# Conditioning pieces, chained token loads and a split projection in a two-layer diffusion step

## The reference

```python
for i in range(DEPTH):
    mp = adaln(c_ctx[None, :], mod_w[i], mod_b[i])      # silu(cond) @ w + b: 6 vectors
    ms = adaln(c, mod_w[i], mod_b[i])
    hp = rmsnorm(xp, norm_mix[i]) * (1.0 + mp[:, 1]) + mp[:, 0]
    ...
    op, st = rglru_mixer(hp, h0, *p)     # or chunk_mlp_mixer; out = (mixed * gate) @ w_out
    xp = xp + mp[:, 2] * op
    hp = rmsnorm(xp, norm_ffn[i]) * (1.0 + mp[:, 4]) + mp[:, 3]
    xp = xp + mp[:, 5] * swiglu(hp, ffn_w_gate[i], ffn_w_up[i], ffn_w_down[i])
```

## Time and profile before

| | us |
|---|---|
| median of 3 runs | 1532.39 (1531.67 to 1532.84) |
| the profiled execution | 1532.15 |
| its span, slowest core (6) | 1530.6 |
| TensorE busy | 1437.0 |
| VectorE busy | 906.6 |
| ScalarE busy | 650.6 |
| GpSimd busy | 225.7 |

### The profile page before, as it was taken

One profiled execution on the slowest core, in us unless ns is written; L12 is line 12 of the kernel. 1 busy time (PEld: TensorE's weight loads), 2 busy tenths in 40 slices (PEclk: granted clock), 3 DMA queues, 4 the chain that ended last, 5 costly groups with the idle time before them and its releaser, 6 DMA issues.

```text
span 1530.6 us, 20044 instructions; the slowest of 8 cores (1516.5 to 1530.6 us)
## 1 busy us (share of the span) xinstructions
PE 1437.0 (94%) x6971; PEld 661.7 (43%) x6971; DVE 906.6 (59%) x1316; ACT 650.6 (43%) x866; POOL 225.7 (15%) x377
## 2 busy tenths in 40 slices
PE   4978996899999999999999999999999999999997
PEld 2433443444444445444444444444444444444444
DVE  1578695458687646528863364538856447744446
ACT  2597996548888234632013032632125013201023
POOL 6011021135231210011111100011110000101000
PEclk9999998999999999999999999999999999999999
DMA  9998368499435873554646754353332535985303
GB/s 176 171 191 129 49 110 193 57 156 146 74 60 86 168 137 55 84 83 70 110 69 97 117 101 72 56 83 56 55 63 47 86 55 93 198 142 87 65 1 110
DMA packets 50182, 151.56 MB, mean 99 GB/s; under 512 B 5410, under 2 KB 11042, under 8 KB 49572
## 3 DMA queue, kind: packets, MB, share of 16 engines
q0 software_dynamic: 45312, 133.32, 53.2%
q1 hardware_dynamic: 4772, 16.96, 3.4%
HBM read 270.94 MB, written 8.42 MB: 183 GB/s over the span
## 4 chain that ended last, share of the span: by engine, by line
PE 79%; DMA 9%; ACT 5%; issue 4%; DVE 3%; POOL 0%; DVEq 0%; ACTq 0%; POOLq 0%
PE pb L110 78%; DMA ringF<-modw 4%; DMA x_fm<-lru_in 2%; ACT h L105 1%; ACT reg L105 1%; ACT L105 1%; DMA x_fm<-xin 1%; DMA ringM<-lru_in 1%; DMA ringF<-ffn_d 1%; DVE x_fm L112 1%; DVE tmpn L112 1%; DMA tff<-lru_w_out 0%; ACT FS L105 0%; ACT x_fm L105 0%; DMA ringM<-lru_w_out 0%
## 5 line engine op out<-in xcount | busy, mean ns | idle before, releaser
L110 PE MATMUL pb<-h,ringF 128*128 128x512 bf16 x2624 | 585.7, 380 | 1.8 <-DVE FS L116 0.9
L110 PEld LDWEIGHTS pb<-h,ringF 128*128 128x128 bf16 x2624 | 255.3, 98 | 311.6 <-issue 9.3
L112 DVE SCALAR_TENSOR_TENSOR x_fm<-pb,modT,x_fm 128x512 f32<-128x512 f32 (+1 forms) x264 | 192.5, 733 | 196.6 <-PE pb L110 191.1
L110 PE MATMUL pb<-FS,ringF 128*128 128x512 bf16 x1312 | 296.6, 383 | 5.0 <-DVE x_fm L112 2.4
L105 ACT ACTIVATE tff<-pb 128x512 f32<-128x512 f32 x176 | 104.8, 596 | 385.7 <-PE pb L110 385.4
L112 DVE SCALAR_TENSOR_TENSOR tff<-tff,pb 128x512 f32<-128x512 f32 x176 | 120.2, 685 | 167.4 <-ACT tff L105 167.3
L110 PEld LDWEIGHTS pb<-FS,ringF 128*128 128x128 bf16 x1312 | 128.5, 99 | 161.8 <-issue 14.5
L116 DVE TENSOR_TENSOR FS<-tff,pb 128x512 bf16<-128x512 f32 x176 | 120.4, 685 | 68.8 <-PE pb L110 65.9
L105 ACT ACTIVATE h<-x_fm 128x1024 bf16<-128x1024 f32 (+2 forms) x86 | 84.2, 994 | 141.0 <-DVE x_fm L112 134.8
L105 ACT ACT_TABLE_LOAD x84 | 107.8, 1283 | 76.9 <-PE pb L110 69.3
L110 PE MATMUL pb<-h,ringM 128*128 128x512 bf16 x548 | 124.1, 380 | 4.3 <-DMA ringM<-lru_in 3.3
(11 more groups left out here) (152 smaller groups left out, 1252.3 us busy)
## 6 DMA issues: line engine op xcount, KB each, us to landing
ringF<-ffn_g POOLq DMA_DIRECT2D x45, 512.0 KB, 5.7
ringF<-ffn_u POOLq DMA_DIRECT2D x45, 512.0 KB, 6.9
ringF<-ffn_d POOLq DMA_DIRECT2D x36, 512.0 KB, 7.1
ringF<-modw POOLq DMA_DIRECT2D x34, 512.0 KB, 8.1
x_fm<-xin SPq DMA_DIRECT2D x4, 2048.0 KB, 14.3
yout<-x_fm SPq DMA_DIRECT2D x12, 512.0 KB, 8.3
ringM<-lru_in POOLq DMA_DIRECT2D x20, 256.0 KB, 5.6
ringM<-lru_w_out POOLq DMA_DIRECT2D x19, 256.0 KB, 5.7
```

Source lines behind the costliest of these rows:

```text
L110: "matmul": lambda e, a, k: e.matmul(*a, **k),
L112: "scalar_tensor_tensor": lambda e, a, k: e.scalar_tensor_tensor(*a, **k),
```

## The change

It does five things: the pieces of the second layer's first conditioning group are spread over `ffn(0, 0)` from its second FFN group on (`mfrom`), not from the first; pieces of layer 1 are assumed to land 3 us later than before (`SL1`); tiles 2 and 3 are loaded, both times, by `load_x4`, eight pieces of 512 KB on SP's queue, each issued after the one before has landed (the second time they were on POOL's queue); tile 1's output projection is cut after six channel blocks (`OSP1`); the priority of tile 1's recurrence goes from 0.8 to 1.0.

```diff
-OSP, OSP1 = 6, 8
+OSP, OSP1 = 6, 6
-P1 = 0.8
+P1 = 1.0
+MF, SL1 = 1, 3.0
+X4 = 3
...
-        wv, wres = ring.load(desc, 1 << 20, prio=prio, slack=SLK if l == 0 and G > 0 else 0.0)
+        wv, wres = ring.load(desc, 1 << 20, prio=prio, slack=SL1 if l == 1 else SLK if G > 0 else 0.0)
...
+    def load_x4(tts, extra=()):
+        prev = list(extra)
+        for tt in tts:
+            for q in range(4):
+                t = P.dma("sp", "xs%d" % tt, lambda e: e.dma_start(out=x_fm[:, tt, 2 * q:2 * q + 2, :], in_=A["d_xin"][tt][:, 2 * q:2 * q + 2, :]),
+                          wr=[XR[(2 * q, tt)], XR[(2 * q + 1, tt)]], extra=prev, nbytes=1 << 19)
+                prev = [t]
...
-                if mods:
+                if mods and grp >= mfrom:
                     mod_piece(*mods.pop(0), prio=2)
...
-    load_x(2, extra=snapshot(KR[0:3] + [GK6]))
-    load_x(3, extra=snapshot(LR[4].all() if M4 else KR[3:6] + [GK6]))
+    if X4 & 1:
+        load_x4((2,), snapshot(KR[0:3] + [GK6]))
+        load_x4((3,), snapshot(LR[4].all() if M4 else KR[3:6] + [GK6]) + [P.tasks[-1]])
...
+    if X4 & 2:
+        load_x4((2, 3), xre)
...
-    ffn(0, 0, segs=((0, (1,)), (1, (0, 1)), (2, (0, 1))) if NSEG == 1 else ((0, (1,)), (1, (1,)), (2, (0, 1))), mods=[(1, 0, kc) for kc in range(KC)])
+    ffn(0, 0, segs=((0, (1,)), (1, (0, 1)), (2, (0, 1))) if NSEG == 1 else ((0, (1,)), (1, (1,)), (2, (0, 1))), mods=[(1, 0, kc) for kc in range(KC)], mfrom=MF)
```

More of the change, by code:

```diff
@@ L617, in emit_program, with ffn @@
     BM = Banks([4, 5, 6])
-    def ffn(l, hf, extra=(), mods=(), ep=1, after=None, segs=((0, (0, 1)), (1, (0, 1)), (2, (0, 1))), kept=None):
+    def ffn(l, hf, extra=(), mods=(), ep=1, after=None, segs=((0, (0, 1)), (1, (0, 1)), (2, (0, 1))), kept=None, mfrom=0):
         mods = list(mods)
@@ L1181, in emit_program @@
     P.prio = 1
-    load_x(2, extra=snapshot(KR[0:3] + [GK6]))
-    load_x(3, extra=snapshot(LR[4].all() if M4 else KR[3:6] + [GK6]))
+    if X4 & 1:
+        load_x4((2,), snapshot(KR[0:3] + [GK6]))
+        load_x4((3,), snapshot(LR[4].all() if M4 else KR[3:6] + [GK6]) + [P.tasks[-1]])
+    else:
+        load_x(2, extra=snapshot(KR[0:3] + [GK6]))
+        load_x(3, extra=snapshot(LR[4].all() if M4 else KR[3:6] + [GK6]))
     P.prio = PB
@@ L1194, in emit_program @@
     xre = snapshot(LR[5].all() + LR[6].all() + GWB)
[L1195 to L1201, removed]
+    if X4 & 2:
+        load_x4((2, 3), xre)
+    else:
+        for tt in (2, 3):
+            if XRP == 0:
+                load_x(tt, extra=xre)
+                continue
+            for q in range(4):
+                P.dma("pool", "xq%d" % (4 * (tt - 2) + q), lambda e: e.dma_start(out=x_fm[:, tt, 2 * q:2 * q + 2, :], in_=A["d_xin"][tt][:, 2 * q:2 * q + 2, :]),
+                      wr=[XR[(2 * q, tt)], XR[(2 * q + 1, tt)]], extra=xre, nbytes=1 << 19, prio=XRP)
     out_proj(0, "d_lru_w_out", (2, 3), BM, ringM)
```

## The result

The changed kernel takes 1540.13 us (median of five runs, 1539.46 to 1544.19), the kernel before beside it 1532.84. The ratio is 1.0053, 95% interval 1.0034 to 1.0072: slower by half a per cent. The prediction said 1515 us, range 1505 to 1530, with 0.10 for slower. It was wrong in sign and outside its range.

The account below looks back on a forecast made before the run. The prediction took TensorE as the bound, standing at `modw` loads before tile 1's FFN. Gains of 12.5 + 1.5 + 1.5 + 2 = 17.5 us from 1532.15 gave 1514.7, with 0.2 to the median 1515 us, range 1505 to 1530.

Parts of the forecast that it names:

- The step that failed: Conditioning loads moved out of the first FFN group return later, covered by two tiles' matmuls per weight: 0 cost.
- Largest term, 12.5 us: Gap before tile 1's FFN: without the piece's wait, projection ends earlier, FFN starts at 284.5; 12.5 us gained, bounds 7 to 15.2.
- Rival E: Tile 1's recurrence: priority 1 delays each block's exponential and root, 2 us a block, 16 us; total 1531 to 1533; chance 0.05.
- Slack, 1.5 gained: Second layer's pieces, matmuls planned 3 us later behind ready FFN groups: 1.5 us gained, bounds 3.4 gained and 1 lost.
- 300 to 380, 1.5 gained: Stretch 300 to 380 us, DMA engines 90% busy: eight loads fewer cut TensorE's idle, 1.5 us gained, bounds 0 and 2.5.
- P1, 2 gained: Tile 1's recurrence at priority 1: one or two ScalarE table loads vanish, 2 us gained, bounds 10 gained and 5.3 lost.
- rival D: ScalarE batches two blocks of tile 1's recurrence, table loads fall by a third: 8 us more gained, 1507; chance 0.12.
- The first chain at 0: First load of tiles 2 and 3, chained at 4.5 us a piece: 0 on the path, lets projection weights land early.
- The second chain at 0: Second load of tiles 2 and 3, chained on SP at 4.5 us a piece: 0, bounds 1 gained and 20 lost.
- Rival C: Chained loads of tiles 2 and 3 too slow, 8.3 us a piece: 1552; losses begin at about 6; chance 0.10.
- B: Gap before tile 1's FFN: TensorE's wait finds another name, gap shrinks by 7 and little else comes: 1525; chance 0.18.
- the most fragile step: Every load and group after 230 us: the planner's new order everywhere else costs no more than the old.

Follow-up runs that it names:

- b_mf: Kernel before, only the first conditioning group's pieces moved to start from the second FFN group of tiles 0 and 1; ratio 1.0082.
- a_g2: Changed kernel with seven conditioning pieces in the third FFN group and the eighth at the head of the second half's FFN; ratio 1.0056.
- a_g2_sq_x1: a_g2_sq with the second load of tiles 2 and 3 again in eight pieces on GpSimd's queue, unchained; 1528.91 us, ratio 0.9950.
- e_cm: Changed kernel with the four loads of the chunk mixer's weights ranked behind the ring loads in GpSimd's order; ratio 1.0047.
- b_p1: Kernel before, only the priority of tile 1's recurrence raised from 0.8 to 1.0; ratio 0.9992.
- b_x4a: Kernel before, only the first load of tiles 2 and 3 made eight chained pieces; ratio 1.0034.
- e_sq: Changed kernel with the squares of tiles 2 and 3 held until the last MS write of tile 1's recurrence; ratio 1.0042.
- b_sl: Kernel before, only the slack of the second layer's pieces set to 3 us instead of 0; ratio 1.0155.
- a_g2_sq: a_g2 with the squares of tiles 2 and 3 also held until the last MS write of tile 1's recurrence; ratio 0.9994.
- e_nosecond: Changed kernel with the second load of tiles 2 and 3 as before, eight unchained loads on GpSimd's queue; ratio 1.0071.
- g2_x0: a_g2 without either chained load and with the priority of tile 1's recurrence back at 0.8; ratio 0.9979.

## Why the prediction was wrong, point by point

**The step that failed**: "They return later, where two tiles' worth of matmuls per weight cover them: 0." Measured: 10.2 us. TensorE stands 3.9 us between 480 and 640 before and 14.1 after, in the mean of the cores. b_mf makes this loss alone. Moving only the pieces on (a_g2) takes 7.8 us off 480 to 515 and adds 4.5 in 515 to 640, where the second chain then holds TensorE; without that chain and with the late squares (a_g2_sq_x1) 6.4 us are left in the two together. The count that was missing is, by these rows, one of slots: what a slot holds and when it comes free. The second group's last part runs beside the last block of the second half's recurrence. There TensorE lives on products with loaded weights: before it has nine nearly in a row, 72 matmuls from 498 to 516. A slot filled with `ffn_d` is four products of eight matmuls, 32 x 216 ns = 6.9 us of work; the same slot filled with a piece is four matmuls, 0.40 us in the trace. "Two tiles' worth per weight" is an average over the group and says nothing of the one place in it where loads cannot keep up. That the moved pieces cause the loss is shown; that they do so by their slots more than by their bytes rests on the issue times above (e_cm) and on no run of its own.

**Largest term, 12.5 us: mis-sized.** The `modw` wait went, the split worked, groups of six stand where they should. From the last write of `MS` to the FFN it took 44.0 us before (253.0 to 296.9) and takes 34.1 now (261.1 to 295.2), 9.9 us less. Of these 8.2 are eaten by a later recurrence. So the failing part is the sentence that put the last write at 252.97 unchanged. b_p1 alone moves it by 6.6 us, b_x4a alone by 4.0, both together 6.1, and e_sq takes 3.6 of these back: with priority 1, close to the 1.2 of the squares and with a switch of table counted 12, ScalarE picks squares of tile 2 amid tile 1's recurrence, and stands there when the chained piece is late. In b_p1, where no piece is late, the four squares (247.69 to 251.57, 3.9 of the 6.6 us) stand ahead of the recurrence's last two steps on ScalarE; in the kernel before they come behind them. Rival E saw half of it, as two microseconds a block of waiting for a table, with chance 0.05.

**Slack, 1.5 gained: wrong in sign.** 13 us lost alone (b_sl). The prediction counted waits on `modw` and held "ring slots held longer" against them at 1 us. In 300 to 380, 8 us are lost in this way: a piece that waits longer for its matmuls keeps a slot of four from the next weight, and that weight's load falls behind GpSimd's own work. The 4.3 us in 480 to 515 have another cause, the order on VectorE. In the changed kernel the first part isn't there (2.5 us standing in 300 to 380), since the pieces left the one-tile group; what the slack costs elsewhere in it wasn't tried.

**300 to 380, 1.5 gained.** Not seen: 2.5 us standing against 2.2 before, 3.7 of 80 without work on the slowest core against 2.5 in the earlier trace rows.

**P1, 2 gained.** From 150 to 262 ScalarE has 25 table loads where it had 24, so none vanished. No gain; rival D is out.

**The first chain at 0: right as a sum by luck, wrong in its parts.** Alone it costs 5 us by the ratio (b_x4a), with the pieces out of the way it gives about 3 us of standing. The estimate of 4.5 us a piece was low. SP's queue of the changed kernel, to be held against the earlier trace rows:

```profile
228.72 27.73 SPq L109 DMA_DIRECT2D x_fm<-xin  x5
...
260.37 12.98 SPq L109 DMA_DIRECT2D x_fm<-xin  x3
```

Four waits in 27.4 us (the fifth issue is the row's last 0.3) are 6.9 a piece, where 4.5 had been taken. The squares that need them stand in ScalarE's queue amid the recurrence, which the prediction had covered only for TensorE's queue ("both tiles are normalised only after tile 1").

**The second chain at 0: wrong, hidden at first.** Its eight issues take 43.94 us in the changed kernel, seven waits of 6.2 each; in a_g2_sq 50.6 us, 7.2 each. Rival C had put the start of losses at 6 us a piece, and the rows fit: at 6.2 a piece removing it gave 0.7 us of standing (e_nosecond), at 7.2 it took 5.2 us of standing from 515 to 575, and the ratio went from 0.9994 to 0.9950. The Trainium skill ("DMA: Bandwidth & Descriptors", the measured table's rule) says to batch to 1 MiB or more; by its fixed and variable cost, fitted there to transfers through GpSimd, a piece is 3.2 us, an estimate from that page. The rule's direction agrees with these rows, 6.2 to 7.2 us a piece of 512 KB beside 12.0 for 2 MB; the size of the estimate doesn't, and the pieces had other transfers beside them.

**Rivals.** B happened in b_x4a and in part in the change (`lru_w_out` for `modw`). C is right for the second load once the pieces are out of its way. D did not happen. E is right in its delay and wrong in its price alone. The sentence on the most fragile step, that the planner's order elsewhere costs no more than the old, named the place of the error without working it out.

**Open.** b_mf's mean span is 15.1 us longer than before: 8.1 us are standing over the whole span and 6.4 matmul time at the lower clock (16.1 against 9.7), some 5 of these in 225 to 380, as in the changed kernel. Why it still comes out slower than the change, which has more edits that cost, wasn't traced. Bytes against slots, as said. Whether g2_x0 and a_g2_sq_x1 differ, and by what. Whether slack 3 still costs with the pieces in the second or third group wasn't tried.

## What to carry to other kernels

When loads are moved, count the slots of the ring at the tightest place they come to, in microseconds of work that a slot holds, and not the average of work per byte. When a wait is taken out of an engine's queue, list what stands next in that queue and when each of these is ready: the edits before it (priority, chains, order of squares) that cost nothing while the wait hid them get their price back. Test each edit of a bundle alone and then with its partner: here the split and priority 1 alone give nothing, the slack and the first chain alone cost 13 and 5 us, and the version with the pieces one group later, late squares and no second chain is 0.5% faster than the kernel before.

## What the runs showed of the hardware

- Eight matmuls that follow a wait of 7.25 us take 3.57 us, against 1.89 in other rows of the same stretch, the granted clock being 0.50 there, the 1.2 GHz level. Before, fillers stood in most such places. A shorter wait is worth less than its length when what comes behind it is real work: 3.7 us of the 8.8 lost are of this kind.
- A load of 512 KB through GpSimd's queue took 8.6 us issued at 492.74 and 26.3 us issued at 506.20, right behind 2.5 MB for the chunk mixer; putting it ahead of them (e_cm) removed its wait of 2.5 us and left the total where it was (1.0047 against 1.0053).
- The x pieces, 512 KB chained on SP's queue, cost 6.2 to 7.2 us from issue to issue beside GpSimd's loads, though a 2 MB transfer on the same queue took 12.0 us: that is 512 KB in 3.0 us, so the chained pieces ran at half of that rate or less.
